# Adding the attention bias on TensorE, inside the score bank, in a two-block transformer kernel

## The reference, cut to what matters

```python
# mix1 (runs twice): 6 plain heads, then 4 differential heads, each two softmaxes
bias = -slopes[:, None, None] * dist                       # |query - key|
s1 = einsum('bqhd,bkhd->bhqk', q1b, k1) * scale + bias
s2 = einsum('bqhd,bkhd->bhqk', q2b, k2) * scale + bias
p = softmax(s1) - lam * softmax(s2)
# even (once): 8 heads, banded:  s = where(valid, s, -1e30), with sink logits
# odd (once): 8 heads, three dilated branches merged: 0 or -1e30, then a table of counts
```

## Time and profile before

| what | value |
|---|---|
| median of 3 runs | 1822.5 us (1818.25 to 1824.02) |
| the profiled execution, its own time | 1816.97 us |
| its span, first to last instruction | 1815.1 us |
| mean granted TensorE clock | 0.964 of full |
| PE / DVE / ACT / POOL busy | 1682.8 / 1246.6 / 1007.7 / 530.6 us |
| the attention with biased rows | 131 to 176 and 520 to 559 (mix1), 1036 to 1082 (even), 1528 to 1601 us (odd) |

### The profile page before, as it was taken

The page is one execution under the profiler, slowest core; times in us unless marked ns, Lnnn a source line. Parts: engine busy times, 40 slices in busy tenths (PEclk is TensorE's granted clock), DMA queues, the critical chain, the costliest instruction groups (busy, mean ns, idle before and its releaser), DMA issues. The chain is left out here.

```text
span 1815.1 us, 30456 instructions
## 1 busy us (share of the span) xinstructions
PE 1682.8 (93%) x10312; PEld 1463.1 (81%) x10312; DVE 1246.6 (69%) x1956; ACT 1007.7 (56%) x1594; POOL 530.6 (29%) x511
## 2 busy tenths in 40 slices
PE   5896899999986999999999967999999999799999
PEld 5785799888865999888888846888888888568888
DVE  5775677756776777667766756776577655857763
ACT  5455466545573666466646555665466536446652
POOL 4040433310311434234420004443144311434430
PEclk9998899999997999999999988999999999789999
DMA  6330355654311556555563302656455654225563
GB/s 231 105 117 24 96 182 185 222 167 143 103 69 36 170 183 201 198 163 186 201 208 128 117 1 97 194 187 209 160 189 188 214 175 139 69 93 193 188 212 102
DMA packets 70793, 274.13 MB, mean 151 GB/s; under 512 B 7872, under 2 KB 9024, under 8 KB 70592
## 3 DMA queue, kind: packets, MB, share of 16 engines
q1 hardware_dynamic: 70272, 271.04, 44.9%
q0 software_dynamic: 448, 2.13, 0.3%
HBM read 272.09 MB, written 1.05 MB: 150 GB/s over the span
## 5 line engine op out<-in xcount | busy, mean ns | idle before, releaser
L782 DVE TENSOR_TENSOR wl<-raw,wh 128x1024 fp32r<-128x1024 f32 (+1 forms) x474 | 627.4, 1324 | 108.7 <-ACT wh L518 102.5
L518 ACT ACTIVATE wh<-raw 128x1024 fp32r<-128x1024 f32 (+1 forms) x474 | 529.2, 1118 | 209.0 <-PE gb L1201 124.8
L1197 PE MATMUL gb<-hx,wh 128*128 128x512 f32 x1540 | 553.8, 399 | 0.0
L1198 PE MATMUL gb<-hx,wl 128*128 128x256 f32 x1540 | 432.2, 281 | 0.0
L1197 PE MATMUL gb<-gux,wh 128*128 128x512 f32 x960 | 341.1, 394 | 0.0
L1197 PEld LDWEIGHTS gb<-hx,wh 128*128 128x128 f32 x1540 | 289.8, 188 | 60.5
L1184 PE MATMUL gb<-hx,wh 128*128 128x256 f32 x1008 | 297.7, 295 | 24.4 <-DVE wl L782 17.0
L1198 PEld LDWEIGHTS gb<-hx,wl 128*128 128x128 f32 x1540 | 291.0, 189 | 7.9
L1185 PE MATMUL gb<-hx,wh 128*128 128x256 f32 x1008 | 286.5, 284 | 0.0
L1186 PE MATMUL gb<-hx,wl 128*128 128x256 f32 x1008 | 286.1, 284 | 0.0
L1198 PE MATMUL gb<-gux,wl 128*128 128x256 f32 x960 | 268.1, 279 | 0.0
(11 more groups left out here) (219 smaller groups left out, 2166.7 us busy)
## 6 DMA issues: line engine op xcount, KB each, us to landing
raw<-in_wa SPq DMA_DIRECT2D x378, 512.0 KB, 3.5
raw<-in_wb SPq DMA_DIRECT2D x96, 704.0 KB, 4.1
x<-in_x SPq DMA_DIRECT2D x1, 1024.0 KB, 4.9
out_x<-x SPq DMA_DIRECT2D x8, 128.0 KB, 3.0
row<-in_row POOLq DMA_DIRECT2D x1, 836.0 KB, 10.2
tab<-in_bias SPq DMA_DIRECT2D x3, 256.0 KB, 4.7
con<-in_const POOLq DMA_DIRECT2D x1, 544.0 KB, 7.1
tab<-in_bias SPq DMA_DIRECT2D x1, 512.0 KB, 5.2
```

Source lines behind the costliest of these rows:

```text
L518: nc.scalar.activation(wh[:, slot, 0:nt * P], raw[:, slot, 0:nt * P], ACT.Copy).then_inc(s_hi, 1)
L782: nc.vector.tensor_tensor(wl[:, slot, 0:nt * P], raw[:, slot, 0:nt * P], wh[:, slot, 0:nt * P].bitcast(f32), ALU.subtract).then_inc(s_lo, 1)
L1197: nc.tensor.matmul(bank[:, :], a, both(k), start=start and k == 0, stop=False)
L1198: nc.tensor.matmul(bank[:, 0:SEQ], b, high(k), start=False, stop=False)
```

## The change

PE multiplies an identity (in mix1 an identity scaled by the head's slope) with the table into the score bank, as one full-array float32 matmul of 512 columns, and accumulates the two score matmuls on it. DVE's biased copy into `pr` goes, and the maximum and the exponentials read the bank. A score bank is free only when the exponentials have read it. The four scaled identities are written by DVE at the start of each mix1, into a buffer that only the feed-forward stages use otherwise; PE waits for the tables at the start of each mixer.

```diff
@@ scores (PE)
-                        pe.wait_ge(m["maxima" if BIASED[kind][r - 2] else "exps"], r - 1)
+                        pe.wait_ge(m["exps"], r - 1)
+                    biased = hs[t].bias is not None
+                    if biased:
+                        if kind == "mix1":
+                            pe.wait_ge(m["slopes"], 1)
+                        nc.tensor.matmul(mb[r % 2][:, :], slope(hs[t].h) if kind == "mix1" else ident, tab[:, 0:512],
+                                         start=True, stop=False)
                     for qt in range(2):
                         last = nc.tensor.matmul(mb[r % 2][:, qt * SEQ:(qt + 1) * SEQ], ...,
-                                                ..., start=True, stop=True)
+                                                ..., start=not biased, stop=not biased or qt == 1)
@@ row_max (DVE)
-                    if h.bias is not None:
-                        if r >= 6:
-                            dve.wait_ge(m["probs_turned"], row_owner(hs, r - 6) + 1)
-                        link(nc.vector.scalar_tensor_tensor(out=pr[:, r % 6, :], in0=tab[:, 0:512], scalar=h.bias,
-                                                            in1=s, op0=ALU.mult, op1=ALU.add))
-                        s = pr[:, r % 6, :]
@@ softmax_exp (ACT)
-                        src = mb[r % 2][:, cs] if h.bias is None else pr[:, r % 6, cs]
+                        src = mb[r % 2][:, cs]
@@ mixer (DVE), ahead of the first unit
+                if kind == "mix1":
+                    if n == 0:
+                        dve.wait_ge(s_con, 64)
+                    for h in heads(kind):
+                        if h.bias is not None:
+                            last = nc.vector.tensor_scalar(slope(h.h), ident, h.bias, None, ALU.mult)
+                    last.then_inc(m["slopes"], 1)
@@ mixer (PE), ahead of the first unit
+                pe.wait_ge(s_tab, T0[n])
@@ new helper
+        def slope(h):
+            return gs[:, h // 2, 1 + h % 2 * P:1 + (h % 2 + 1) * P]
```

More of the change, by code:

```diff
@@ L230, in build_program @@
                  "probs probs_turned probsT attn_out mix_hi mix_lo").split()
-        OWN = {"mix1": ("rotated roped attn_copied mix_psum mix_sbuf gate_sigs gates_ready k_packed level_scores diag_copied level_copied totals q_up k_up stats "
+        OWN = {"mix1": ("slopes rotated roped attn_copied mix_psum mix_sbuf gate_sigs gates_ready k_packed level_scores diag_copied level_copied totals q_up k_up stats "
                         "stats_log stats_rsd c_copied").split(),
@@ L316, in before @@
                 n += outputs(kind, w, k)
-        BIASED = {k: [hd.bias is not None for hd in heads(k) for _ in hd.rows] for k in W}
         MISC = mb[2]
+        def slope(h):
+            return gs[:, h // 2, 1 + h % 2 * P:1 + (h % 2 + 1) * P]
         def bank_of(kind, u):
@@ L1286, in scores @@
                                                 y[part, qc * SEQ + qt * P:qc * SEQ + (qt + 1) * P],
-                                                y[part, kc_ * SEQ:(kc_ + 1) * SEQ], start=True, stop=True)
+                                                y[part, kc_ * SEQ:(kc_ + 1) * SEQ], start=not biased, stop=not biased or qt == 1)
                     last.then_inc(m["scores"], 1)
```

## The result

| | before | after |
|---|---|---|
| median of 19 runs each | 1823.25 us (1815.08 to 1831.12) | 1842.35 us (1821.15 to 1851.30) |
| ratio, 95% interval | | 1.0059 (1.0033 to 1.0085), some +11 us |
| profiled execution: time, span, granted clock | 1816.97, 1815.1, 0.964 | 1827.82, 1826.0, 0.975 |

The change makes the kernel slower, +10.9 us in the profiled execution. The executions of the changed kernel lie in two groups, 8 of 19 between 1821 and 1831 us and 11 between 1842 and 1851; before has no such groups. The ratio leaves out the six slowest executions, above 1848 us, and the median does not. So no single number describes the loss: the mean of the short group is 3.5 us above the median before, that of the long group 24 us, and the +11 us of the ratio lies between the groups, where there is no execution. The profiled execution is one of the short group.

The account below looks back on a forecast made before the run. PE, busy for 93% of the span, was taken to bound the kernel. Mix1 +9.2, even -1.5 and odd -1.4 gave +6.3, plus 1 for uncounted links: +7.5 us, a median of 1830.0 us, range 1817 to 1840.

Parts of the forecast that it names:

- the cause that it names: In mix1, where PE is the path, full-array bias matmuls add PE time and end the two rows' side-by-side run.
- The bias matmul: On PE, each full-array float32 bias matmul takes 0.86 us at full clock; 32 of them take 27.5 us.
- The lost side-by-side run: In mix1, a bias matmul between a differential head's two rows ends their overlap: +3.0 us a head at full clock.
- The stronger wait: In mix1's heads 8 and 9, waiting for the exponentials of row r-2 before reusing a bank costs nothing.
- Slopes: At mix1's start, four 128x128 products for the scaled identities, mostly hidden behind ACT's weight copies: +0.3 us.
- The mix1 tail: Heads 8 and 9 and what follows in mix1: -0.8 us with full clock kept, +1.7 without.
- If PE starts at half clock for the 6 us that it did before, add 2.5: Mix1's heads 8 and 9: 6 us at half clock turn the +0.6 us there into +3.1.
- Held or lost: Whether PE's clock stays full after idle times of 1.9 (mix1), 2.0 (even), 2.7 us (odd): yes, yes, no.
- Even: The even mixer: -1.5 us with full clock kept, up to +2.0 without; the sum took -1.5.
- Odd: The odd mixer: -1.4 us with the clock at half, -4.9 at full; the sum took -1.4.
- rival (d): Faster: a fuller PE keeps full clock through odd's last 21 us; -5 us, 1817.5 us; chance 0.14.
- rival (b): PE falls to half clock at all these places in mix1, even and odd: +15 us, 1837.5 us; chance 0.20.

Follow-up runs that it names:

- e1: Changed kernel with the bias on PE in the two mix1 stages only, even and odd keeping DVE's biased copy; ratio to the kernel before 1.0116.
- e3: Changed kernel with both bias matmuls of a mix1 head issued first, then its four score matmuls; ratio to the kernel before 0.9993.
- e9: Kernel before, DVE's copies kept, plus a full-array matmul per biased row that scores overwrite, in mix1 a head's two first; ratio to before 1.0041.
- e5: Kernel before with one edit: a biased row's score bank is released after its exponentials, not its maximum; ratio to before 1.0008.
- e6: Changed kernel with 14 short unused matmuls put into PE's wait ahead of head 5's transposes in mix1; ratio to the kernel before 1.0073.
- e4: Kernel before, DVE's copies kept, plus a full-array matmul ahead of each biased row's scores, which overwrite it; ratio to before 1.0098.
- e7: Changed kernel with the bias on PE in even and odd only, from tables rounded to fp32r, mix1 as before; ratio to the kernel before 0.9943.

## Why the prediction was right, and where its terms were not

It forecast slower by 7.5 us (its terms give 6.3 + 1 = 7.3). The ratio says 11, within its range of 1817 to 1840 us, and the median of all executions says 19, 1842.35 us, just above that range. The direction comes from the cause that it names, and e1, e3 and e9 show this cause. The size is in part luck: the terms do not all fit, and there is no one size to hit.

- **The bias matmul, 0.86 us of PE.** Right: 131.72 to 132.67 is 0.95 with the change of shape.
- **The lost side-by-side run, +3.0 us a head in mix1.** Right: 2.98 us at head 6, +4.9 at the c output's copy (5.1 said). e3 shows it from the other side.
- **The stronger wait costs nothing.** Right, e5. **Slopes +0.3:** 8 x 222 ns, and DVE waits there anyway; too small to be seen.
- **The mix1 tail, -0.8 with the clock held, +1.7 without.** The held case was right in kind: in the first stage 0 up to L1322 and then -1.3 us on the last heads, and e6 has both stages at +3.5 and +3.9 us from head 6 on, where the terms give 4.6. The lost case was mis-sized: in the step "If PE starts at half clock for the 6 us that it did before, add 2.5" the half clock lasted 13 us, and the tail took 6.5 us more up to L1322 in place of 3.1. That makes both mix1 stages +13.8 us, where the sum had +9.2 and 14.2 as its far end.
- **Held or lost, chosen by the length of the wait.** This step failed. The prediction took the clock as held in mix1 and even because the new waits, 1.9 and 2.0 us, are shorter than the 2.59 us that had not cost it. A wait of 1.86 us held it in one mix1 and lost it in the other, one of 2.44 us at head 7 held it in the profiles before and after and lost it in those of e1, e3, e4 and e7, and 1.86 us lost it in even.
- **Even, -1.5 expected, +3.2 measured.** Up to head 5 as said for the lost clock (-0.2, then +2.3; 0 and +1.9 said). "Held" was the wrong choice, and the 1.96 us wait near the end, which I had not looked at, now cost the clock too, where 2.59 us before had not the earlier trace rows.
- **Odd, -1.4 expected, -6.1 measured.** Sum and head 4 as said (-1.3 and -1.9; -1.5 and -2.2 said). The half clock behind it was short, so head 5 is at -3.3, and the case of rival (d), transposes and products behind head 7 at a higher clock, came in part: -2.5 us, which the unchanged code of e1 also got.

So two misses of 4.7 us each, in even and odd, cancelled by luck, and mix1's 4.6 went into the sum. The 11 long executions are worse than rival (b) with its +15: +19 to +28 us. The prediction had no term for executions that differ from each other.

## What to carry to other kernels

Before moving an elementwise step to PE as an identity matmul, ask in which order the matmuls then stand: one full-array matmul between two that use different halves of the array ends their overlap, and putting all full-array ones first keeps it. Pay for the table in one rounded pass if its values allow that; 0.86 us a row was break-even in even and odd together, one pass was 0.57% faster. Where PE waits in the middle of a stage, treat the clock as two outcomes, and look at many executions, not at one. And before you credit an edit with a few us of a stage, look at the same stage in kernels whose code there is the same, and compare from the point where the edit begins.

## What the runs showed of the hardware that was not expected

- A busy PE did not get its clock back: 27.0 of 28 us busy at 0.50 in e1 and in e4, and 19.0 of 20 in e7, where the 48-partition rows run side by side and nothing was added in mix1. In e3 it was back within 4 us behind the same wait. Why, the runs do not say.
- Equal waits ended differently: 1.86 us in the first and second mix1 of one execution, once with the clock held, once not, and 2.44 us ahead of head 7, held in two profiles and lost in others.
- Accumulating score matmuls at partitions 0 and 64 run side by side in different banks as plain ones do: 8 records in 1.14 us.
